# Pairwise modulation in the first layer of a hybrid diffusion step: loads, splits and token tiles in a new order

## The reference

```python
mod = silu(c) @ w_mod[l] + b_mod[l]               # 3 x 1024: shift, scale, gate; once for c, once for c_ctx
shift, scale, gate = jnp.split(mod, 3, axis=-1)
xn = _rmsnorm(h, w['norm_g']) * (1.0 + scale[..., None, :]) + shift[..., None, :]
a_in, a_z, b_in, b_z, q_lat, kv_lat, k_rope, c_z, g_all = _split_cols(xn @ w['w_in'])
# Fourier mixing of a_in, pooling of b_in, latent attention of q_lat, kv_lat and k_rope,
# each gated and projected, merged by sigmoid gates, one output product, gated residual add
```

## Time and profile before

| | us |
|---|---|
| median of 3 executions | 2223.52 |
| lowest, highest | 2221.91, 2224.67 |
| the profiled execution | 2222.64 |
| its span | 2220.4 |
| TensorE busy (13185 matmuls) | 2131.5 |
| VectorE, ScalarE, GpSimd busy | 1090.4, 886.7, 653.6 |

### The profile page before, as it was taken

The page is one execution under the profiler, slowest core; times in us unless marked ns, Lnnn a source line. Parts: engine busy times, 40 slices in busy tenths (PEclk is TensorE's granted clock), DMA queues, the critical chain, the costliest instruction groups (busy, mean ns, idle before and its releaser), DMA issues.

```text
span 2220.4 us, 35875 instructions
## 1 busy us (share of the span) xinstructions
PE 2131.5 (96%) x13185; PEld 2035.3 (92%) x13185; DVE 1090.4 (49%) x2823; ACT 886.7 (40%) x2223; POOL 653.6 (29%) x560
## 2 busy tenths in 40 slices
PE   7999999999999999999999999999999999999997
PEld 5899878888899999999989997888888999999997
DVE  2441268888864667663162314888886111120213
ACT  2521267777831212113152214777777112111312
POOL 1323122322322234333441311222323223343342
PEclk8999999999999999999999999999999999999999
DMA  9811000000343333224255100000005111111232
GB/s 275 267 33 31 26 1 1 1 1 1 121 155 85 95 83 100 78 63 143 74 197 163 40 1 26 1 2 1 1 14 192 48 36 48 40 46 39 65 124 85
DMA packets 194622, 155.67 MB, mean 70 GB/s; under 512 B 8637, under 2 KB 186001, under 8 KB 193425
## 3 DMA queue, kind: packets, MB, share of 16 engines
q1 hardware_dynamic: 194448, 153.38, 22.2%
HBM read 124.89 MB, written 28.48 MB: 69 GB/s over the span
## 4 chain that ended last, share of the span: by engine, by line
PE 84%; DVE 7%; ACT 4%; issue 3%; DMA 1%; POOL 0%; SPq 0%; DVEq 0%; POOLq 0%; ACTq 0%
PE ps L1607 23%; PE ps L1609 23%; PE ps L1608 23%; PE ps L1798 5%; PE ps L1823 3%; PE ps L1824 2%; DVE partmax L1450 1%; DVE probsT L1463 1%; PE ps L1617 1%; DVE kT L1420 1%; ACT kT L879 1%; PE ps L1841 1%; ACT probsT L848 1%; DVE xn_high L1201 1%; ACT probs L832 1%
## 5 line engine op out<-in xcount | busy, mean ns | idle before, releaser
L1607 PE MATMUL ps<-xn_high,split_br 128*128 128x384 f32 x1584 | 531.8, 336 | 0.0
L1609 PE MATMUL ps<-xn_high,split_br 128*128 128x384 f32 x1584 | 529.5, 334 | 0.0
L1608 PE MATMUL ps<-xn_low,split_br 128*128 128x384 f32 x1584 | 529.3, 334 | 0.0
L960 ACT ACTIVATE sigmoids<-ps 128x384 f32<-128x384 f32 x144 | 70.4, 492 | 613.5 <-PE ps L1609 613.5
L1608 PEld LDWEIGHTS ps<-xn_low,split_br 128*128 128x128 f32 x1584 | 297.5, 188 | 0.0
L1607 PEld LDWEIGHTS ps<-xn_high,split_br 128*128 128x128 f32 x1584 | 297.4, 188 | 0.0
L1609 PEld LDWEIGHTS ps<-xn_high,split_br 128*128 128x128 f32 x1584 | 297.3, 188 | 0.0
L1002 POOL TENSOR_TENSOR split_br<-raw,split_br 128x1024 fp32r<-128x1024 f32 x82 | 198.2, 2418 | 320.4 <-ACT split_br L693 320.4
L1463 DVE TENSOR_TENSOR probsT<-ps,probsT 128x384 fp32r<-128x384 f32 x384 | 213.1, 555 | 70.1 <-ACT sum_inv_rows L855 42.7
L832 ACT ACTIVATE probs<-ps,negmax 128x384 f32<-128x384 f32 (+1 forms) x400 | 229.1, 573 | 29.3 <-DVE negmax L1456 28.7
L1798 PE MATMUL ps<-ident,probs 128*128 128x128 f32 x1168 | 197.5, 276 | 31.0 <-DVE kT L1420 15.8
(11 more groups left out here) (227 smaller groups left out, 4197.4 us busy)
## 6 DMA issues: line engine op xcount, KB each, us to landing
raw<-in_w_in SPq DMA_DIRECT2D x74, 512.0 KB, 3.9
raw<-in_w_mod SPq DMA_DIRECT2D x48, 512.0 KB, 5.0
park_high<-xn_high SPq DMA_DIRECT2D x6, 1536.0 KB, 6.4
park_low<-xn_low SPq DMA_DIRECT2D x6, 1536.0 KB, 10.6
xn_high<-park_high SPq DMA_DIRECT2D x2, 4608.0 KB, 16.0
rows<-in_x_sample SPq DMA_DIRECT2D x16, 512.0 KB, 6.8
raw<-in_w_out SPq DMA_DIRECT2D x16, 512.0 KB, 6.5
rows_mid<-rows SPq DMA_DIRECT2D x9, 512.0 KB, 2.6
```

The costliest lines, as they stand in the source:

```text
L960: a.activation(sig[:, ch, :], PS[:, b, 0:CH], ACT.Sigmoid).then_inc(bank_free[b], 1)
L1607: mm(out, wh, xh, start=first, stop=False)
L1608: mm(out, wh, xl, start=False, stop=False)
L1609: return mm(out, wl, xh, start=False, stop=last)
```

## The change

Layer 0 only, up to the end of the token phase; the token phase of layer 1 keeps its order.

- The modulation blocks are loaded and multiplied in pairs (f, 8 + f). A pair fills one of two PSUM banks (3 and 4), and is copied, turned, biased and made a scale by itself, so `scale_ready` counts up by feature block.
- Between the pairs TensorE turns chunk 0's feature blocks (TURN_IN_MODS), and makes p = 0 for tiles 0 to 2 together, one feature block at a time (`tok_step`, TOK_IN_MODS). Then chunk 1 in the same way, its turns two blocks ahead.
- The order of tiles becomes (0,0..5), (1,0..2), (0,6..8), (1,3..8), written (p,t); chunk 2 is turned inside (1,1).
- SP's order: pair 0, rows 0 to 2, pairs 1 to 5 with tok 0 after pair 2 and tok 1 after pair 3, rows 3 to 5, pairs 6 and 7, tok 2 to 5, rows 6 to 8, and then the three constants. The ring rule is the same.
- ScalarE and GpSimd put the splits of tok 0 to 5 between the values of chunks 0 and 1; the squares of chunk 1 stand ahead of chunk 0's last value.

```diff
 OUT_DEST = (0, 1, 2, 3, 4, 5, 0, 1)
 NORM_IN_OUT = {5: (0, 0, 3), 6: (0, 3, 6), 7: (0, 6, 8)}
-NORM_IN_ROWS = {1: 1, 4: 2}
+NORM_IN_TOK = ({(1, 1): 2}, {(0, 1): 1, (0, 4): 2})
+MODS = [m for f in range(KF) for m in (f, KF + f)]
+TOK_ORDER = ([(0, t) for t in range(2 * CT)] + [(1, t) for t in range(CT)] + [(0, t) for t in range(2 * CT, TT)]
+             + [(1, t) for t in range(CT, TT)],
+             [(p, t) for p in range(2) for t in range(TT)])
+TURN_IN_MODS = {1: (0, 1), 2: (2,), 3: (3,), 4: (4,), 5: (5,), 6: (6,), 7: (7,)}
+TOK_IN_MODS = {5: (0, 1), 6: (2, 3), 7: (4,)}
+DVE_IN_MODS = {1: (0,), 2: (1,), 3: (2,), 4: (3,), 5: (4,), 6: (5, 6), 7: (7,)}
+def tok_item(l, p, t):
+    return TOK_ORDER[l].index((p, t))
...
+    def tok_unit(l, u):
+        c0, width = TOK_UNITS[u]
+        split_unit(("tok", l, u), [(0, KF, wcols(w_in, l, c0, width))], 2 + u if u < 2 else 4 + u,
+                   (l, "tok", tok_item(l, int(u >= 2), TT - 1)))
+    for i, m in enumerate(MODS):
+        unit(("mod", 0, m), [(0, KF, wcols(w_mod, 0, m * P))], None, (0, "mod", i // 2))
...
-            split_unit(("tok", l, u), [(0, KF, wcols(w_in, l, c0, width))], 2 + u if u < 2 else 4 + u,
-                       (l, "tok", (TT if u < 2 else 2 * TT) - 1))
+        for u in range(0 if l else 2, len(TOK_UNITS)):
+            tok_unit(l, u)
...
-        load_units(sp, 0, 6)
+        load_units(sp, 0, 2)
         for t in range(CT):
             load_rows(t)
-            load_units(sp, 6 + 3 * t, 9 + 3 * t)
-        load_units(sp, 15, unit_at[("tok", 0, 2)])
+        load_units(sp, 2, unit_at[("mod", 0, 6)])
+        for t in range(CT, 2 * CT):
+            load_rows(t)
+        load_units(sp, unit_at[("mod", 0, 6)], unit_at[("tok", 0, 5)] + 1)
+        for t in range(2 * CT, TT):
+            load_rows(t)
         for dst, src in ((q_scale, "q_scale"), (edge, "edge"), (pool_mat, "vec_zero")):
             sp.dma_start(dst[:], tab[src]).then_inc(S("const_in"), 16)
-        for t in range(CT, 2 * CT):
-            load_rows(t)
-        load_units(sp, unit_at[("tok", 0, 2)], unit_at[("tok", 0, 4)])
-        for t in range(2 * CT, TT):
-            load_rows(t)
         for l in range(DEPTH):
...
-                if f == 0:
-                    act.wait_ge(S("scale_ready"), l + 1)
+                if l == 0 and ch == 0:
+                    act.wait_ge(S("scale_ready"), f + 1)
+                elif l and f == 0:
+                    act.wait_ge(S("scale_ready"), KF + 1)
...
+        norm_values(0, 0, 0, 2)
         split_high(("tok", 0, 0))
-        norm_values(0, 0, 0, 4)
+        norm_values(0, 0, 2, 3)
         split_high(("tok", 0, 1))
-        norm_values(0, 0, 4, KF)
+        norm_values(0, 0, 3, KF - 1)
+        squares(0, 1, square_rows[:])
+        norm_values(0, 0, KF - 1, KF)
+        roots(0, 1)
+        split_high(("tok", 0, 2))
+        split_high(("tok", 0, 3))
...
+            if l:
+                squares(l, 1)
+                roots(l, 1)
+            else:
+                for t in range(CT):
+                    tok_rows(0, t)
+                norm_values(0, 1, 0, KF)
+                split_high(("tok", 0, 4))
+                split_high(("tok", 0, 5))
+            squares(l, 2, beside_squares)
             roots(l, 2)
...
+            for p, t in TOK_ORDER[l][CT if l == 0 else 0:]:
+                tok_rows(p, t)
+                if (p, t + 1) in NORM_IN_TOK[l]:
+                    norm_values(l, NORM_IN_TOK[l][p, t + 1], 0, KF)
...
+        norm_low(0, 0, 0, 2)
         split_low(("tok", 0, 0))
-        norm_low(0, 0, 0, 4)
+        norm_low(0, 0, 2, 3)
         split_low(("tok", 0, 1))
         norm_low(0, 0, 4, KF)
+        split_low(("tok", 0, 2))
+        norm_low(0, 1, 0, 4)
+        split_low(("tok", 0, 3))
+        norm_low(0, 1, 4, KF)
+        split_low(("tok", 0, 4))
+        split_low(("tok", 0, 5))
+        norm_low(0, 2)
...
+        for f in range(KF):
+            b = filled(dve, 0, "mod", f)
+            v.tensor_copy(mod_flat[0:2, f % 2, :, :], PS[0:2, b, 0:2 * P].rearrange("c (s m) -> c s m", s=2))\
+                .then_inc(bank_free[b], 1)
+            if f == 0:
                 norm_factors(0, 0)
                 norm_rows(0)
...
+            b = filled(dve, 0, "modt", f)
+            v.tensor_tensor(modT[:, 0, f:KF + f + 1:KF, :], PS[:, b, 0:4].rearrange("p (s c) -> p s c", c=2),
+                            vecT[:, f:KF + f + 1:KF].unsqueeze(2).broadcast_to([P, 2, 2]), ALU.add)\
+                .then_inc(bank_free[b], 1)
+            read_out(dve, 0, "modt", f)
+            v.tensor_scalar(scaleT[:, f, :], modT[:, 0, KF + f, :], 1.0, vecT[:, 48 + f:49 + f], ALU.add, ALU.mult)\
+                .then_inc(S("scale_ready"), 1)
+            for ff in DVE_IN_MODS.get(f, ()):
+                norm_dve(0, 0, ff, ff + 1)
...
+            if l == 0:
+                norm_dve(l, 1)
+                norm_factors(l, 2)
...
+        def tok_step(ch, k):
+            low_done(pe, KF * ch + k + 1)
+            for t in range(ch * CT, (ch + 1) * CT):
...
+        for f in range(KF):
+            mod_part(f, 0)
+            if f:
+                mod_turn(f - 1)
+            mod_part(f, 1)
+            for ff in TURN_IN_MODS.get(f, ()):
+                norm_turn(0, 0, ff, ff + 1)
+            for k in TOK_IN_MODS.get(f, ()):
+                if k == 0:
+                    pe.wait_ge(S("split_low"), split_k[("tok", 0, 1)] + 1)
+                tok_step(0, k)
+        mod_turn(KF - 1)
+        for k in range(5, KF):
+            tok_step(0, k)
+        for k in range(KF + 2):
+            if k < KF:
+                norm_turn(0, 1, k, k + 1)
+            if k >= 2:
+                tok_step(1, k - 2)
...
+            for p, t in TOK_ORDER[l][2 * CT if l == 0 else 0:]:
+                if t == 0:
+                    pe.wait_ge(S("split_low"), split_k[("tok", l, 5 if p else 1)] + 1)
```

More of the change, by code:

```diff
@@ L113, in bank_plan @@
     add(0, "vec", 6, 1, 1)
-    add(0, "mod", 0, 6, 16)
-    add(0, "modt", 6, 1, 1)
+    add(0, "mod", 3, 2, KF)
+    add(0, "modt", 5, 1, KF)
     add(0, "norm", 6, 2, NCH * KF)
@@ L395, in hybrid_step @@
     vec_rows = r.put("vec_rows", [P])
-    mod_flat = r.put("mod_flat", [16, P])
+    square_rows = Region(starts["br"][0], 4096).put("square_rows", [D])
+    mod_flat = Region(starts["ws"][0] + 14336, 2048).put("mod_flat", [2, 2, P])
     PS = nc.alloc_psum_tensor("ps", [P, 8, 512], F32)
@@ new lines, in _, with tok_rows @@
+        norm_values(0, 0, 3, KF - 1)
[4 more added lines that the diff above has]
+        split_high(("tok", 0, 3))
+        for l in range(DEPTH):
+            def tok_rows(p, t):
+                b = filled(act, l, "tok", tok_item(l, p, t))
+                if t % CT == 0:
+                    act.wait_ge(S("xhat"), 9 * l + (3 if p == 0 else 6 if l == 0 and t == 0 else 9))
+                if l and t == 0:
+                    for ch in ((1, 2) if p else (0,)):
+                        act.wait_ge(S(f"mid_out{ch}"), 16 * CT)
+                if p == 0:
+                    ins = a.activation(atok[:, t, :], PS[:, b, 0:256], ACT.Copy)
+                else:
+                    s = t if t < 8 else 9
+                    a.activation(qlat[:, t, :], PS[:, b, 0:QR], ACT.Copy)
+                    ins = a.activation(kvk[:, s, 0:LATENT - QR], PS[:, b, QR:LATENT], ACT.Copy)
+                ins.then_inc(bank_free[b], 1)
+            beside_squares = PS[:, 3:5, :].rearrange("p b n -> p (b n)")
+            filled(act, l, "norm", KF - 1)
+            if l:
+                squares(l, 1)
+                roots(l, 1)
+            else:
+                for t in range(CT):
[4 more added lines that the diff above has]
+            squares(l, 2, beside_squares)
+            roots(l, 2)
+            for p, t in TOK_ORDER[l][CT if l == 0 else 0:]:
+                tok_rows(p, t)
+                if (p, t + 1) in NORM_IN_TOK[l]:
+                    norm_values(l, NORM_IN_TOK[l][p, t + 1], 0, KF)
+                if l and p == 0 and t in (2, 5):
+                    for u in ((2, 3) if t == 2 else (4, 5)):
+                        split_high(("tok", l, u))
+                if p == 1 and t in (3, 5):
+                    split_high(("feat", l, t // 5))
@@ L1609, in three_pass, with mod_part, mod_turn @@
             return mm(out, wl, xh, start=False, stop=last)
-        def mod_item(m):
-            b = pe_takes(pe, 0, "mod", m)
-            nu = unit_at[("mod", 0, m)]
+        def mod_part(f, part):
+            b = pe_takes(pe, 0, "mod", f) if part == 0 else item(0, "mod", f)[0]
+            nu = unit_at[("mod", 0, MODS[2 * f + part])]
             arrived(pe, nu)
             for k in range(KF):
-                ins = mm(PS[0:2, b, 0:P], silu_c[:, k, :], raw[:, nu % 4, k, :], start=(k == 0), stop=(k == KF - 1))
+                ins = mm(PS[0:2, b, part * P:(part + 1) * P], silu_c[:, k, :], raw[:, nu % 4, k, :], start=(k == 0),
+                         stop=(k == KF - 1))
+            if part:
```

(22 more changed lines are left out.)

80 lines of the change are left out of this document (15 added, 65 removed).

## The result

| | us |
|---|---|
| changed kernel, median of 6 | 2231.08 (2226.35 to 2232.85) |
| kernel before beside it | 2221.74 |
| ratio, 95% interval | 1.0038, 1.0027 to 1.0049 |
| the profiled execution, its span | 2232.85, 2230.9 |

The change makes the kernel slower by 0.4% (9.3 us); a second series of it (the first experiment) gives 0.2% (5.6 us against its own before, 2222.41). The forecast was 2228.

A forecast was written before the change was run, and what follows sets the result against it. TensorE, busy 96% of the span, was taken as the bound, so only its waits in layer 0 could change the time. 2222.6 + 5 (later last latent read) + 0.9 gave 2228.5, stated as 2228; range 2209 to 2237.

The forecast's parts named there:

- Early rows: Layer 0, chunk 0: rows 0 to 2 land at 13.5 instead of 34.0, normalised rows at 20.6.
- The ring: Modulation loads: slots behind token blocks open only after GpSimd's low halves, so modulation ends some 18 us later.
- the walk: Layer 0 followed in time through loads, splits and turns: last latent read at 140.4 before any clock loss.
- Chunk 1's rows waiting out GpSimd's split: VectorE's row operations of chunk 1 wait out GpSimd's split of token block 2; third row ready at 71.9.
- ScalarE's reads behind the squares: Before the first latent tile: tile 3's bank is read only behind three squares and a root, 87.6; three us of wait.
- The clock: After TensorE's second idle stretch (68 to 72), turns and steps at half clock cost 4 us, giving 144.5.
- the walk without the clock: Layer 0's last latent read at 140.4, with no loss for low clock counted.
- the middle of 140.4 and 144.5: Last latent read taken as 142.5, between the ends without and with clock loss: 5 us later than 137.5.
- What follows repeats the order of before: Behind layer 0's last latent read nothing changes, so gain or loss is how far that read moves from 137.46.
- Rival 1: Layer 0's load waits don't form and the overlap pays: last latent read 126 to 133, 2211 to 2219 us; chance 0.28.
- the three transposes of a feature block: TensorE's turning of one feature block, put at about 0.4 us in the sum of work at full clock.

The follow-up runs named there:

- the first experiment: The changed kernel measured again with no edit: median 2227.96 us, ratio 1.0022 to the kernel before.
- Side blocks: The changed kernel with token weight blocks 0 and 1 loaded to places of their own, outside the four-slot ring: 2221.05 us, ratio 0.9994 to the kernel before.
- split later: The changed kernel with GpSimd's splits of token blocks 2 and 3 two feature pairs later in its order: 2226.90 us, ratio 1.0019 to the kernel before.
- read first: The changed kernel with ScalarE reading Fourier tiles 3 to 5 ahead of chunk 2's squares: 2225.90 us, ratio 1.0017 to the kernel before.
- Hold clock: The changed kernel with 20 and 16 unread matmuls in TensorE's waits before chunk 1's turns and the first latent tile: 2226.71 us, ratio 1.0022.
- after again: Second series and profile of the changed kernel, no edit: 2227.96 us, ratio 1.0022 to the kernel before.
- after: The changed kernel's first series and profile, against the kernel before: 2231.08 us, ratio 1.0038.
- all three: The changed kernel with token blocks 0 and 1 outside the ring, splits of blocks 2 and 3 later, tiles 3 to 5 read before the squares: 2219.43 us, 0.9988.

## Why the prediction was near

- **Early rows.** Landing 13.5, normalised 20.6 forecast; 13.15 and 20.2 measured.
- **The ring.** First split at 30.7, second 41.4, pair 5 at 47.2 to 48.8, last turn 63.5 forecast; 27.8, 38.7, 45.4 and 62 measured. The waits formed where they were put (idle 41.9 to 45.4 forecast, 39.5 to 42.85 measured), 1.5 to 3 us sooner: the forecast counted a part of pair 2 at half clock and ended it at 28, and it ended at 25.07 with the granted clock at 1.00 from 14 to 26. No late landing showed either (that the walk added none was the author's estimate): the block issued at 38.70 was used 4.15 us later, where the walk had 4.0. "Side blocks" shows the mechanism: without it the last latent read falls to before's.
- **Chunk 1's rows waiting out GpSimd's split.** 71.9 forecast, 69.3 measured, with the 2 us of delay as forecast; "split later" shows it.
- **ScalarE's reads behind the squares.** Three us of wait forecast before the first latent tile, 2.96 measured; "read first" shrinks it to 1.58, where GpSimd's last split ends it.
- **The clock, and luck.** 0.5 somewhere in 68 to 82 forecast, 68 to 78 measured. But the 4 us put on this one stretch don't follow from the forecast's figures (6 us at 2.7 us a block instead of 1.4 lose 3), and it cost 1.7. "Hold clock", whose rows were ready at the same time (69.3), shows the parts. Against the walk without the clock (140.4), the rows came 2.6 us sooner. From them to the first latent matmul the walk had 15.7 us; at full clock it took 17.5 (1.8 more), and with the first low stretch 19.2 (1.7 more). The second low stretch, behind the wait at 86 to 88.5, stood in no step of the forecast; with it the first latent read came 6.3 us later instead of 4.8 (1.5 more). The rest is 0.2 less. That makes 2.2 us, beside the 2.1 that came from taking the middle of 140.4 and 144.5. So 142.5 forecast and 142.63 measured agree by errors that cancel, and the same kernel also gave 143.07 and 140.38.
- **The term that was missing.** "What follows repeats the order of before" is true of the order, not of the time: the profiled execution loses 4.9 us at 642 and 0.4 later. In "after again" 2227.96 stands beside the forecast 2228, again by some luck: the forecast added 5 us to a before of 2223.5, the median of three executions, and measured were 5.6 over 2222.4.

Rival 1 (the overlap pays) failed by the chain it named: the split stands behind value, cast and low half, so the ring opened at 27.8 and 38.7. It named 28 and 37 as the limits; the first was met, the second missed by 1.7 us. That this second block alone held pairs 5 to 7 up is argued from the queue's longest wait; the runs took both blocks out at once.

A small thing in its sums: the three transposes of a feature block are put at 0.4 us, while the row named gives 8.7 / 16 = 0.54, a part of it at half clock (0.50 up to 64).

What stays open: how often the late chain is long in this kernel. It was in 2 of the 8 profiles of the changed kernel and its variants without the fixed order (after, "hold clock"); no run shows that the change makes it likelier, nor that it doesn't. Three of the first series' six times are above 2231, none of the second's nine, and two of the eleven of "split later".

## What to carry to other kernels

A ring slot opens with the slowest step in front of it (here a load went out at 38.70, behind a split that ended at 38.67). Before putting blocks that go through a long chain (value, cast, split) between blocks that only TensorE frees, walk the queue's times; a small place of their own was worth 6.3 us here. A wait of about 3 us can cost twice where work follows it densely, once as idle time and once by the low clock behind it (here 0.50 in 68 to 78 behind a wait of 3.34 us, 0.57 in 88 to 92 behind one of 2.96): place waits where the engine has little to do behind them, or order the reads so that they vanish. When one wait is taken away, look for the next: the wait for VectorE's rows became one for its last low half, and that one for GpSimd's splits. And before crediting an edit with 3 us read from one profile, profile the unchanged kernel again: here it moved by 2.7 by itself.

## What the runs showed of the hardware

- A few hundredths of a us can decide 2 us: where GpSimd's split starts 3.53 us (or 3.47) into VectorE's chain, the chain takes 6.32; where it starts 3.58 to 3.69 into it, 4.23 or 4.24 (2 and 7 profiles). With the long chain TensorE's wait of 1.1 us becomes 3.2, and the clock falls behind it (0.51 in 648 to 654 of the first profile, 0.51 in 645 to 652 of "hold clock"). What moved the start in those two is not shown.
- VectorE's casts and scalings with one input were held by GpSimd's subtraction as long as its operation with two: a cast took 2.61 us and a low half 2.58, where 0.36 and 0.56 is usual ("all three"), and three scalings 4.17 instead of 2.08.
- Unread matmuls in two waits kept the granted clock at 1.00 in 68 to 78 and 88 to 92, where it had been 0.50 and 0.57. The same wait (2.96, 2.95 and 2.96 us) was followed by a low stretch in two profiles of the changed kernel (0.57 and 0.50 in 88 to 92) and by none in the third (1.00).
